# A hybrid decoder step on one core: norm weights move to ScalarE's copies, 1/rms into a diagonal on TensorE, and the gated linear attention's output becomes one VectorE operation per head

## What is computed

```python
def rmsnorm(x, g):
    y = x * lax.rsqrt(jnp.mean(jnp.square(x), -1, keepdims=True) + EPS)
    return y * g

z   = rmsnorm(x, norm_mix) @ w_in                       # 2048 x 3920: latent attention | linear attention
q   = rmsnorm(rmsnorm(cq, norm_q_lat) @ w_uq, qk_gain_q)   # per head 128 + 64 rotary
k   = concat(k_nope * qk_gain_k[:128], rope(k_rope * qk_gain_k[128:])) * inv_rms
mla = softmax(q @ k.T * scale) @ v                      # prompt causal; sample over paged latents
o   = gated linear attention, 4 heads of 128 x 256, chunked
gla = rmsnorm(o, norm_gla_out) * silu(r)                # per head of 256
h   = x + concat(rmsnorm(mla, norm_mla_out), gla) @ w_out
h   = h + peer(rmsnorm(h, norm_ffn))                    # 8 heads, top 16 of 128 x 128 experts:
                                                        # per token and head 16 rows of peer_u and of peer_v
y   = h + sigmoid(rmsnorm(h, norm_ple) @ w_ple_gate) * (p @ w_ple_proj)
```

## Time and profile before

| | |
|---|---|
| median of three runs | 4408.99 us (4402.73 to 4420.45) |
| the profiled execution's own time | 4402.15 us |
| its span, first to last instruction | 4400.3 us |
| VectorE busy | 3337.7 us, 76% |
| TensorE busy | 2226.7 us, 51% |
| ScalarE busy | 490.1 us, 11% |
| DMA | 1606.6 MB, mean 365 GB/s |

### The profile page before, as it was taken

How to read it: one execution, slowest core, us unless ns; L and a number is a source line. 1 busy time by engine, 2 the same in 40 slices (tenths; PEclk the granted TensorE clock), 3 DMA queues, 4 the chain that set the end, 5 groups by cost and what they waited for, 6 DMA issues and landing times.

```text
span 4400.3 us, 23443 instructions
## 1 busy us (share of the span) xinstructions
PE 2226.7 (51%) x8006; PEld 1309.9 (30%) x8006; DVE 3337.7 (76%) x3712; ACT 490.1 (11%) x917; POOL 2235.1 (51%) x1232
## 2 busy tenths in 40 slices
PE   8999715324898492789852438800000380000746
PEld 3456403213384131367641212800000130000312
DVE  0230699898568997968889865699999879987772
ACT  1220102221001001222112011000000100000000
POOL 0000365634232466567785742545768647877440
PEclk9999856557999796767765669955555695555877
DMA  8667889988998999889998999988899999999996
GB/s 309 235 228 283 332 345 357 362 330 323 420 419 342 412 423 384 349 328 367 395 392 326 363 389 421 401 347 328 369 414 389 400 422 422 422 404 422 421 396 213
DMA packets 262973, 1606.64 MB, mean 365 GB/s; under 512 B 28051, under 2 KB 50131, under 8 KB 92934
## 3 DMA queue, kind: packets, MB, share of 16 engines
q0 software_dynamic: 176448, 1268.30, 71.2%
q1 hardware_dynamic: 84518, 327.82, 19.7%
q10 hardware_dynamic: 1888, 9.03, 0.5%
HBM read 1561.93 MB, written 42.56 MB: 365 GB/s over the span
## 4 chain that ended last, share of the span: by engine, by line
PE 34%; DVE 30%; POOL 14%; DMA 12%; issue 7%; ACT 2%; another core or an unknown queue 0%; SPq 0%; DVEq 0%; ACTq 0%; POOLq 0%
PE bank L791 15%; POOL ring L2407 13%; DVE total L1890 10%; DVE ring L1865 10%; PE bank L1201 5%; DMA ring<-in_peer_u,idx_all 4%; PE bank L1164 4%; DMA ring<-in_peer_v,idx_all 4%; PE bank L845 1%; PE bank L765 1%; POOL front L2389 1%; PE bank L995 1%; PE bank L1035 1%; PE bank L1009 1%; PE bank L915 1%
## 5 line engine op out<-in xcount | busy, mean ns | idle before, releaser
L2407 POOL DMA_INDIRECT ring<-in_peer_v,idx_all x576 | 1086.7, 1887 | 747.5 <-DVE total L1890 346.3
L1865 DVE CUSTOM_DVE_ANT_0 ring<-ring,xrow 128x2048 f32<-128x2048 f32 x576 | 1298.5, 2286 | 205.8 <-DMA ring<-in_peer_u,idx_all 203.3
L1890 DVE SCALAR_TENSOR_TENSOR total<-ring,gate_all,total 128x2048 f32<-128x2048 f32 x571 | 1342.0, 2350 | 144.7 <-DMA ring<-in_peer_v,idx_all 119.5
L2407 POOL DMA_INDIRECT ring<-in_peer_u,idx_all x576 | 1050.7, 1824 | 756.0 <-DVE dots L1865 387.5
L791 PE MATMUL bank<-front 128*128 128x512 f32 (+3 forms) x2048 | 897.7, 596 | 76.4 <-ACT front L1996 71.8
L765 PE MATMUL bank<-ident,front 128*128 128x128 f32 (+1 forms) x320 | 61.8, 369 | 1375.5 <-DVE front L1290 1298.7
L791 PEld LDWEIGHTS bank<-front 128*128 128x128 f32 (+1 forms) x2048 | 357.2, 179 | 606.7 <-issue 602.1
L765 PEld LDWEIGHTS bank<-ident,front 128*128 128x128 f32 (+1 forms) x320 | 50.5, 201 | 1394.0 <-DVE front L1290 1295.2
L1164 PE MATMUL bank<-front 128*128 128x128 f32 (+2 forms) x1536 | 257.3, 330 | 11.1 <-DMA front<-in_peer_w_q 7.6
L1164 PEld LDWEIGHTS bank<-front 128*128 128x128 f32 x1536 | 241.0, 193 | 29.0 <-DMA front<-in_peer_w_q 11.4
L1201 PE MATMUL bank<-ring 128*128 128x490 f32 x384 | 165.6, 579 | 2.1 <-ACT front L1996 2.1
(11 more groups left out here) (305 smaller groups left out, 2806.8 us busy)
## 6 DMA issues: line engine op xcount, KB each, us to landing
front<-in_w_in SPq DMA_DIRECT2D x64, 980.0 KB
front<-in_w_out SPq DMA_DIRECT2D x48, 1024.0 KB
front<-in_peer_w_q SPq DMA_DIRECT2D x48, 1024.0 KB
front<-in_w_ple_gate SPq DMA_DIRECT2D x48, 1024.0 KB
ring<-in_w_in POOLq DMA_DIRECT2D x12, 1960.0 KB, 10.0
front<-in_w_uq SPq DMA_DIRECT2D x6, 1536.0 KB, 9.0
ring<-in_peer_u,idx_all POOLq DMA_INDIRECT x576
ring<-in_peer_v,idx_all POOLq DMA_INDIRECT x576
```

What stands on the lines that cost most here:

```text
L1865: e.tensor_tensor_reduce(out=ring[:, b, :], in0=ring[:, b, :], in1=xrow[:, t % 2, :], scale=1.0, scalar=0.0, op0=ALU.mult, op1=ALU.add, ac ...
L1890: e.scalar_tensor_tensor(out=total, in0=ring[:, b, :], scalar=c1, in1=total, op0=ALU.mult, op1=ALU.add).then_inc(s("summed"), 1)
L2407: e.indirect_dma_start(out=ring[:, k % RING, :], out_offset=None, in_=a[("peer_u", "peer_v")[side]][0], in_offset=bass.IndirectOffsetOnAxi ...
```

## The change

1. The gains of `x`, `mix` and `ple` are no longer broadcast. A small table `gains_t` (128 partitions x 3 x 16), prepared on the host as a layout of the three gains, is loaded once. The broadcast loads of `norm_mix`, `norm_mla_out`, `norm_gla_out` and `norm_ple` go.
2. For these three norms VectorE writes only `inv_diag = ident * 1/rms` (128 x 128). TensorE forms `row.T @ inv_diag` in place of the transpose, straight from the loaded row; ScalarE puts the gain on while it copies, 16 operations of 128 columns with a per-partition scale in place of 4 of 512. The `ffn` norm stays as it is.
3. The linear attention's output: ScalarE squares it from PSUM; VectorE makes one operation per head, `PSUM * 1/rms * gsil`; the gain is in the table with `norm_mla_out`, so columns 1024 to 2047 get it in ScalarE's copy.
4. The key gain's first 128 columns are multiplied into the query gain once; the products at L1382 and L1359 go.
5. Waits move: what waited for `normed` because the row was overwritten next waits for `nt_transposed`; what waited for `gla_o_sb` waits for `gla_o_ready`; TensorE waits for the gated output of tile t - 1 before the output products of tile t.
6. All five order tables are written anew.

```diff
@@ CHAIN_BEFORE_PIECE (128 entries; entries up to step 61: 81 before, 75 after)
-    245, 247, 255, 257, 258, 258, 258, 258, 258, 258, 262, 262, 262, 262, 262, 267, 267, 267]
+    184, 191, 191, 191, 191, 201, 202, 204, 209, 212, 212, 212, 212, 219, 219, 221, 221, 221, 221]
@@ ROWS_BEFORE (714 entries before, 705 after), where the second group's mixer ends
-    166, 166, 166, 169, 169, 199, 199, 199, 204, 204, 237, 238, 238, 238, 239, 239, 239, 239, 239, 239, 239, 239, 240,
+    173, 176, 176, 199, 208, 208, 208, 208, 239, 239, 239, 239, 239, 239, 239, 240, 240, 240, 240, 240, 240, 240, 240,
@@ sync, slabs
-                        e.wait_ge(s("normed"), NORMS["x", GROUPS[int(name[4:])][k - SLABS + MT]] + 1)
+                        e.wait_ge(s("nt_transposed"), 4 * (NORMS["x", GROUPS[int(name[4:])][k - SLABS + MT]] + 1))
@@ sync, loads
+            e.dma_start(gains_t[:, :, :], a["gains_t"]).then_inc(s("consts_loaded"), 16)
-                    e.dma_start(G, down(a["norm_mix"][0])).then_inc(s("gain_loaded"), 16)
-                e.dma_start(g_go, down(a["norm_gla_out"][0])).then_inc(s("gla_w_loaded"), 16)
-                e.dma_start(G[:, 0:H_MLA * DV], down(a["norm_mla_out"][0])).then_inc(s("gain_loaded"), 16)
-                    e.wait_ge(s("normed"), NORMS["mix", tiles[-1]] + 1)
-                e.dma_start(G, down(a["norm_ple"][0])).then_inc(s("gain_loaded"), 16)
@@ tensor, norm_transposes
-                            src = H[:R, sl, k * P:(k + 1) * P] if use == "mix" and k >= 8 else Y[:R, k * P:(k + 1) * P]
-                            mm = e.transpose(norm_bank(n, m)[:, j * P:j * P + R], src, ident[:R, :R])
+                            cols = slice(k * P, (k + 1) * P)
+                            row = Y[:R, cols] if use == "ffn" else in_rows(t)[:R, cols] if use == "x" else H[:R, sl, cols]
+                            out = norm_bank(n, m)[:, j * P:j * P + R]
+                            if use == "ffn" or use == "mix" and k >= KD // 2:
+                                mm = e.transpose(out, row, ident[:R, :R])
+                            else:
+                                mm = e.matmul(out, row, inv_diag[:R, :R], start=True, stop=True)
@@ tensor, linear_attention
+                        if t:
+                            e.wait_ge(s("gla_o_ready"), t)
@@ vector, norm_rows
-                    if (use, t) in GAINS:
-                        yield
-                        e.wait_ge(s("gain_loaded"), 16 * (GAINS.index((use, t)) + 1))
-                    src = in_rows(t)[:R, :] if use == "x" else H[:R, sl, 0:width]
-                    e.scalar_tensor_tensor(out=Y[:R, 0:width], in0=src, scalar=inv, in1=G[:R, 0:width],
+                    if use != "ffn":
+                        e.tensor_scalar(inv_diag[:R, :R], ident[:R, :R], inv, None, ALU.mult).then_inc(s("normed"), 1)
+                        yield
+                        continue
...
@@ vector, gla
-                e.tensor_copy(go[:R, 0:512], gla_out_at(t, 0)[:R, :])
-                e.tensor_copy(go[:R, 512:1024], gla_out_at(t, 2)[:R, :]).then_inc(s("gla_o_sb"), 1)
-                yield
                 e.wait_ge(s("gla_rms"), t + 1)
                 link(e.reciprocal(GIS[:R], GRS[:R]))
-                gv = go[:R, :].rearrange("p (h n) -> p h n", h=H_GLA)
-                link(e.tensor_tensor(gv, gv, GIS[:R].unsqueeze(2).to_broadcast([R, H_GLA, GV]), ALU.mult))
-                link(e.tensor_tensor(gv, gv, g_go[:R, :].unsqueeze(1).to_broadcast([R, H_GLA, GV]), ALU.mult))
-                e.tensor_tensor(go[:R, :], go[:R, :], gsil[:R, :], ALU.mult).then_inc(s("gla_o_ready"), 1)
+                for h in range(H_GLA):
+                    cols = slice(h * GV, (h + 1) * GV)
+                    ins = e.scalar_tensor_tensor(out=go[:R, cols], in0=gla_out_at(t, h)[:R, (h % 2) * GV:(h % 2 + 1) * GV],
+                                                 scalar=GIS[:R, h:h + 1], in1=gsil[:R, cols], op0=ALU.mult, op1=ALU.mult)
+                ins.then_inc(s("gla_o_ready"), 1)
@@ scalar, norm_squares
-                        e.copy(xt[:, 4 * q:4 * q + 4, sl * P:sl * P + R], four(norm_bank(n, m), R)).then_inc(s("nt_evacuated"), 1)
+                        if use == "ffn":
+                            ins = e.copy(xt[:, 4 * q:4 * q + 4, sl * P:sl * P + R], four(norm_bank(n, m), R))
+                        else:
+                            for j in range(4):
+                                k = 4 * q + j
+                                gain = gains_t[:, ("x", "mix", "ple").index(use), k:k + 1]
+                                ins = e.activation(xt[:, k, sl * P:sl * P + R], norm_bank(n, m)[:, j * P:j * P + R], ACT.Copy, scale=gain)
+                        ins.then_inc(s("nt_evacuated"), 1)
@@ scalar, mixer
-                    e.wait_ge(s("gla_o_sb"), t + 1)
+                    e.wait_ge(s("gla_out_psum"), (t + 1) * H_GLA)
```

49 lines of the change are left out of this document (28 added, 21 removed), and 64 rows, old and new, of tables (CHAIN_BEFORE_PIECE, ROWS_BEFORE).

## The result

The changed kernel takes 4420.5 us (median of 20 runs), the kernel before 4411.0 us beside it: a ratio of 1.0021, 95% interval 1.0011 to 1.0030, so 9 us slower where 25 us faster was forecast (within the range, on the wrong side). The same program run again, with the first of the experiments, gave 1.0024 (1.0012 to 1.0036). The profiled execution has a span of 4430.7 us; it was the longest of the 20. A second profile of the same program has 4405.1 us, so landmarks of both are given where it matters.

A forecast was written before the change was run, and what follows sets the result against it. No engine full overall: TensorE bounds until 466 us, the second group's mixer until 1370, then VectorE and DMA pace the rows. -2 -8 -14 -1 = -25 on 4402.15 gives 4377, 4384 against the median; range 4345 to 4425.

The forecast's parts named there:

- The first stage, -2 us: To 475 us, TensorE's stretch: dearer products against the saved norm and a shorter w_out wait; -2 us, bounds -6 and +4.
- The stand of 10.4 us for w_out: TensorE's wait for w_out slabs at 323 us: 6 of 10.4 us taken as gone, bounds 0 and 10.4.
- the 4 us that I had allowed: Sign that the forecast is right: GpSimd's first gather list comes within 4 us of 475.
- ScalarE: Norm evacuations: four small operations 0.95 to 1.1 us for one 0.585 copy; +0.5 us per exposed norm, the rest covered.
- The products: TensorE's products for transposes: +3.5 +0.9 +1.9 to 475 us, +2.3 +3.5 before the second route; tail 4.5 for 2.26 us.
- The norms and the gains' loads: Before 1370 us, mixer and next x norms -4.1 each; later, mixer norms 4, embedding norms nothing, 3.5 MB fewer bytes 5 us.
- The gated output, -8.6 us in the second stage: Tiles 1 and 2, 475 to 1370 us: -3.1 each on VectorE and about 1.2 of waiting for ScalarE, -8.6 us.
- The new order, +5 us: 475 to 1370 us: seven to nine rows put ahead of the path, 16 to 21 us without VectorE idle time; 5 taken.
- The third stage, -14 us: 1370 to 4295 us: 9 of 15 us from VectorE, 5 of 8.9 from DMA bytes; -14, bounds 0 and -24.
- hidden: Rival, 0.25: VectorE and byte savings after 1370 us vanish, rows put ahead eat those from 475 us; -7 us, 4402.
- Slower: Rival, 0.15: rows put ahead delay the second route, doubled transposes add, w_out stall stays; +12 to +38, middle 4434.
- second list at or after 1370 us: Sign that the forecast is wrong: GpSimd's second expert list no earlier than 1370 us, rows ahead costing in full.

The follow-up runs named there:

- the run with the products alone: Kernel before with 200 of its 320 transposes of normed rows made fp32 products with the identity, nothing else changed: 1.0042 (1.0026 to 1.0057).
- the run with plain rows: Kernel before, its order kept, x, mix and ple rows scaled by 1/rms alone, gains and their seven broadcast loads left out: 0.9959 (0.9944 to 0.9974).
- the run with the gated output: Kernel before, its order kept, linear attention's output in one operation per head from PSUM, its gain omitted, key gain folded into query gain: 1.0018 (1.0005 to 1.0031).

## Why the prediction was wrong, point by point

- **The first stage, -2 us.** The stand of 10.4 us for w_out at 323 us went altogether: in the chain of the kernel after, where the state's store and the reload of the mixer rows now stand ahead, the projection runs without a break, and in the second profile its norm rows are stored 4.3 us earlier than before. The price of TensorE's products was about right: 6.3 us in the sum, and the first list 4.6 us late in the run with the products alone. The step that failed is one that the sum did not have: the first list was no longer released by the route but by the ahead pieces, which the new order had put behind. It came 4.6 to 5.0 us later, just outside the 4 us that I had allowed.

```profile
295.85 5.93 DMA s_dram<-front
...
316.50 30.90 PE bank L796 x72
```

- **ScalarE.** Four small operations at 0.95 to 1.1 us: measured 1.14. By the figure of the Trainium skill (ScalarE: Activation LUTs, What ACT_TABLE_LOAD costs) they would have been 1.26, an estimate; the measured time lies between. For the changed kernel the term held: beside its products TensorE stands 1.8 us more than before for banks. The cost would have come with transposes, 1.05 us a norm on all norms and 13 us in the run, which the prediction did not ask since it had products.
- **The products.** The terms of the sum (3.5, 0.9, 1.9, 2.3, 3.5, and 2.2 in the tail) come to 14 us; measured 18 in the old order. In the new one they and the diagonal cost 8 more than transposes of scaled rows, net of 13 us that VectorE has more to do there and of TensorE's 11 us longer stands for ScalarE. Two terms were too small. The third stage had none at all, and the embedding's 80 products alone cost 10 us. In the tail 16 products took 7.08 us for 2.26 where I had 4.5: I took a product as twice a transpose, and at the lower clock and 64 columns it was three times. By Perfetto Trace Analysis of the Trainium skill, Optimizing Tensor Performance (Transposes), a transpose should not be made by a standard matmul; that rule, which I had set aside since the norm's 2.35 us seemed worth more, was the better guide: with transposes kept the kernel before beats the run with products alone, and in the new order the runs with transposes beat those with the diagonal.
- **The norms and the gains' loads.** Right, and too cautious: with only 13.1 us off VectorE and 6.8 MB fewer the run gained 18 us. As far as one run tells, the discounts for the third stage (9 of 15, 5 of 8.9) and nothing at all for the embedding's norms were too large.
- **The gated output, -8.6 us in the second stage and a share of the same 8.6 in the third, each with 2.8 us of key products.** This is the step that failed most: +8 us measured where the sum had some 20 to gain (with what it did for w_out). The VectorE time was as forecast (0.477 us an operation, 48.8 us in all); what failed was to credit it to the path, at no price for the transfers behind it. I wrote of the stores only that they start earlier and never asked what they would then stand behind: rows that the old output's gap had kept away, 6.8 MB of them behind tile 3, where 10 to 13 us were lost. The rows of before had a hint: DMA at 0.91 to 0.95 in those stages, and gains of 0.5 to 1 MB on SyncE's queue that landed in 10.7 to 16.4 us.
- **The new order, +5 us.** Wrong in sign: it brings the changed operations 12 us. It does put the second mixer late, as feared: the load of its z rows at 592 us for 578, the second list at 1379 to 1384 us, a wait of 76 us. Most of that is won back soon: the 351st row request, near 1740 us, is 8 and 2 us late in the two profiles. Which of the five tables does it was not tried.
- **The third stage, -14 us, 9 from VectorE and 5 from bytes.** It held for the norms (the run with plain rows) and failed for the gated output, for the reason above. The rival "hidden" had the stream held by DMA; behind tile 3 what DMA held was the mixer.
- **Rivals.** None of them is the one that came. "Slower" had the doubled transposes and a late second route, and both are there (12 to 38 us was the price, 9 to 11 the result), but it had VectorE's rows in the place of the landings. The listed sign "second list at or after 1370 us" came, but it is not what tells the loss: with the gated output alone the second list stayed at 1369.9 and the kernel lost 8 us.

## What to carry to other kernels

Time taken off the busiest engine is worth what the next wait of that engine allows: before crediting it, look which transfer ends that wait and whether the idle stretch now removed was what kept the DMA engines free for it. An engine's busy share of 75% hides both kinds of place. A pause of known length, put in at one place, tells which kind it is; it needs a run of its own for each version and place. A step moved to another engine is to be priced as a pipeline with the buffers between (here two banks), not as one operation beside another. And a written order belongs to the operations it was made for: here each set of operations was slowest with the other's tables, so an operation tried in a foreign order is not yet priced for its own.

## What the runs showed of the hardware that was not expected

The same 1865 records of products of the attention of tiles 3 and 4 stand between two landmarks in every kernel of the old order, and the stretch between them took from 403 to 424 us. Windows of the kernel before, of the run with the gated output, and of that run with the state store's wait moved (columns as above):

```profile
1877.00:2286.00 409.00, 340.69 (x1865) 277.50 (x1865) 328.12 (x269) 76.23 (x140) 304.12 (x171) 0.71 0.92 367
```

```profile
1873.00:2297.00 424.00, 356.08 (x1865) 290.52 (x1865) 328.75 (x269) 76.12 (x140) 307.81 (x169) 0.68 0.89 355
```

```profile
1871.00:2274.00 403.00, 333.58 (x1865) 271.32 (x1865) 328.25 (x269) 76.37 (x140) 314.24 (x171) 0.73 0.94 373
```

VectorE does the same work in all three; the mean granted clock of TensorE is 0.71, 0.68 and 0.73, its busy time follows, and so does the length. The engine works here in short pieces with idle time between.

The difference goes with the chip more than with the kernel. Two kernels on one chip have 409 and 410 us, two on a second 403 and 406, three on a third 412 to 424 and four on a fourth 415 to 420. The kernel before itself goes the same way: medians of 4400.4 and 4401.9 us on the first two chips and of 4412.7 and 4414.7 on the other two, with a mean clock over the whole run of 0.7186 twice, 0.7174 and 0.7172. So 12 us between two traces, more than what the change did, can be the chip alone. Ratios to the kernel before on the same chip carry every verdict here, and single landmarks only where several kernels agree.

The clock is a small rival of the +8 us as well. Over the 29 runs of the kernel before on the chip of the gated output's run, the time falls by 2.8 us for each 0.001 of mean clock, and the runs with the gated output have 0.0011 less in the mean. By that estimate 3 of the 8 us go with the clock; whether as cause or as consequence no run shows.

A product in fp32 of 128 columns cost TensorE twice a transpose in warm clock, as the earlier trace rows had it. In the tail, with 64 columns and at the lower level, it cost three times as much (7.08 for 2.26 us), and the same in the run with products with the identity. No rows of the kernel before had shown that; how much of it is the clock and how much the 64 columns was not taken apart.
